# Three norms on row-wide tiles instead of one column per token, in a fused two-block layer (one core)

## The chip, the core and the metric

The kernel runs on one core of a Trainium2 chip. The metric is the device time of one execution in microseconds (us), and lower is better. The engines are named as in the profile: PE (TensorE matmuls), PEld (its weight loads), DVE (VectorE), ACT (ScalarE), POOL (GpSimd) and SP (SyncE, which issues most DMAs).

## The reference, cut to what matters

Two blocks run one after the other on 512 tokens of 1024 features: an RWKV-7 branch beside sparse latent attention, then a convolution, memory attention and gated feed-forward block. The change touches only the start of the attention branch:

```python
def rmsnorm(x, g):
    xf = x.astype(jnp.float32)
    y = xf * lax.rsqrt(jnp.mean(xf * xf, axis=-1, keepdims=True) + NORM_EPS)
    return (y * g.astype(jnp.float32)).astype(x.dtype)
...
    xn = rmsnorm(x, norm_g)
    p = xn @ w_in
...
    c_q = rmsnorm(q_down, q_norm_g)         # 256 features
    c_kv = rmsnorm(kv_down, kv_norm_g)      # 128 features, the latent keys
    q = (c_q @ w_uq).reshape(B, T, ATTN_HEADS, HEAD_DIM)
    q_idx = (c_q @ w_qidx).reshape(B, T, IDX_HEADS, IDX_DIM)
    k_idx = layernorm(k_idx_raw, kidx_g, kidx_b).astype(f32)   # 64 features, the selection keys
```

## The kernel before, in words

Activations lie with features on the 128 partitions and the 512 tokens along the free axis. Every large product is cut into weight units of 1024 x 256, each split into a high and a low part: ACT writes `w_hi` (line 1209), DVE writes `w_lo` (line 1665; for later units POOL does, line 1156), and PE runs three products for each chunk of 128 features (lines 392 to 394). Two slots hold the units in turn. The waits of PE for `hi_ready` and `lo_ready` stand in `next_unit`.

Each engine runs a list written out by hand; semaphores join the lists, and no engine changes its order. Units 0 to 2 (`qd`, `kvi`, `wa`) use the input before its norm; from unit 3 (`r`, half 0) on, the operand is the normed input, made chunk by chunk: DVE scales (line 1692), ACT rounds to the high part (line 1255), DVE subtracts (line 1703). PE takes unit `r` chunk by chunk as these become ready, then computes the selection queries (`index_queries`, line 510), then takes unit 4 (`k`, half 0).

A norm's sum over features is a sum over partitions, which PE must make. `column_sums` (line 433) multiplies the squares, as weights, by a single column of ones, so that the 512 sums come out as 4 columns of 128 tokens on the partitions. DVE scales, adds epsilon and inverts these 128 x 4 numbers (`token_root`, lines 1755 and 1757), ACT takes the root (line 1220), and `spread` (line 383) sends them through PE again, so that each token's factor stands on all partitions. This is done for the query down-projection (`ss_q`, `rs_q`), the latent keys (`ss_kv`, `rs_kv`) and the selection keys (`ki_var`, `rs_ki`). PSUM has 8 banks, which PE takes in a ring.

What stands in the lists near the three norms: on DVE, the norm of the queries is ahead of `split_lo(3)`, the low part of unit `r`; that of the latent keys is ahead of chunks 6 and 7 of the normed input; that of the selection keys is ahead of the scaling of the queries (line 1801) and of `split_lo(4)`, the low part of unit `k`. On ACT, the root of the selection keys is ahead of a tanh and of `split_hi(4)`, the high part of unit `k`.

Of the kernel before, what the change touches and what calls it, by code (L numbers as in the profile page):

```python
# [18 lines left out]
ALU = mybir.AluOpType  # L19
# [3 lines left out]
P = 128  # L23
D = 1024
T = 512
CH = D // P
NT = T // P
HD = 64
# [99 lines left out]
def build(nc, dram, out):  # L128
# [3 lines left out]
    with ctx:  # L132
        base = -(-nc.sbuf_base // 32) * 32

        def at(name, offset, shape, dt=F32):
            return nc.alloc_sbuf_tensor_at(name, [P] + shape, dt, offset=base + offset)
# [22 lines left out]
        R0 = 133504  # L159
# [5 lines left out]
        raw_lo = at("raw_lo", R0 + 16384, [CH, T], F32R)  # L165
        sq_x = at("sq_x", R0 + 32768, [CH, T])

        ar = at("ar", R0, [NI, 2, T])
# [156 lines left out]
        def _(pe):  # L325
# [146 lines left out]
            def third_step(u, m, k):  # L472
                if k == 0:
                    pe.wait_ge(lo_ready, u + 1)
                elif k == 4:
                    pe.wait_ge(sem("sq_q"), 2)
                    column_sums("ss_q", [prep[m][:, 0:T] for m in range(2)])

# [7 lines left out]
            pe.wait_ge(sem("sq_kv"), 1)  # L486
            column_sums("ss_kv", [prep[2][:, 0:T]])
            pe.wait_ge(sem("tok_q_ready"), 1)
            spread("rs_q", tok_rs)

            def index_norms(k):
                pe.wait_ge(sem("xn_ready"), k + 1)
                if k == 4:
                    pe.wait_ge(sem("ki_sq"), 1)
                    column_sums("ki_var", [prep[3][:, 0:T]], slice(0, HD))
                elif k == 5:
                    pe.wait_ge(sem("tok_kv_ready"), 1)
                    spread("rs_kv", tok_mix)
                elif k == 7:
                    pe.wait_ge(sem("tok_ki_ready"), 1)  # L500
                    spread("rs_ki", tok_ki)

# [92 lines left out]
            def attention_start():  # L595
                pe.wait_ge(sem("dsa_w"), 16 * 3)
                for i in range(NI):
                    b = bank(("q", i))
                    for m in range(2):
                        mm = nc.tensor.matmul(b[:, :], wuq[:, m, i * P:i * P + P], qd[:, m, :], start=m == 0, stop=m == 1)  # L600
                    done(mm, ("q", i))
                decay_and_rate(1)
                norms_spread(1)
                strict_upper(0)
                evacuated(pe, "rs_kv")
                transposes("ckv_tok", [ckv[:, t * P:t * P + P] for t in range(NT)])
                for i in range(NI):
                    evacuated(pe, ("q", i))
                absorbed_query(0)
                absorbed_query(1)  # L610
                scores(0)
                key_bonus(1)
# [582 lines left out]
        def _(act):  # L1195
# [69 lines left out]
            hi_chunks((3, 4), "xn")  # L1265
            root(tok_rs, "tok_q_ready")
            hi_chunks((4, 5), "xn")
# [6 lines left out]
            A(prep[3][:, 0:T], kidx[:, :], ACT.Square).then_inc(sem("ki_sq"), 1)  # L1274
            root(tok_mix, "tok_kv_ready")
            hi_chunks((6, CH), "xn")
            root(tok_ki, "tok_ki_ready")
            A(tmp[2][0:32, 0:T], tmp[2][0:32, 0:T], ACT.Tanh).then_inc(sem("tanh_ready"), 1)
# [364 lines left out]
        def _(dve):  # L1643
# [109 lines left out]
            def token_root(key, t, scale, eps, name):  # L1753
# [3 lines left out]
                V.reciprocal(t, t).then_inc(sem(name + "_var"), 1)  # L1757

            token_root("ss_x", rs_x, 1.0 / D, NORM_EPS, "tok_x")
            evacuated(dve, "rs_x")  # L1760
# [13 lines left out]
            for m in range(2):  # L1774
# [4 lines left out]
            input_normed(3)  # L1779
            token_root("ss_q", tok_rs, 1.0 / 256, NORM_EPS, "tok_q")  # L1780
            split_lo(3)
# [10 lines left out]
                 ("wa", 0, 0))  # L1792
            token_root("ss_kv", tok_mix, 1.0 / P, NORM_EPS, "tok_kv")
            input_normed(6)
            input_normed(7)
            lo_chunk(CH - 1, "xn")
            token_root("ki_var", tok_ki, 1.0 / HD, LN_EPS, "tok_ki")
            b = take(dve, "rs_q")
            for m in range(2):
                evacuated(dve, ("qd", 0, m))  # L1800
                ins = V.scalar_tensor_tensor(qd[:, m, :], qd[:, m, :], pcol("q_norm_g", m), b[:, :], ALU.mult, ALU.mult)
                ins.then_inc(sem("cq_ready"), 1)
            dve.wait_ge(sem("cq_ready"), 2)
            release("rs_q")
            split_lo(4)

            def latent_keys():
                evacuated(dve, ("kvi", 0, 0))
                b = take(dve, "rs_kv")
                evac(V.scalar_tensor_tensor(ckv[:, :], ckv[:, :], pcol("kv_norm_g"), b[:, :], ALU.mult, ALU.mult), "rs_kv")  # L1810

            def index_keys():
                evacuated(dve, "ki_mean")
                b = take(dve, "rs_ki")
                evac(V.scalar_tensor_tensor(kidx[:, :], kidx[:, :], pcol("kidx_g"), b[:, :], ALU.mult, ALU.mult), "rs_ki")
                evacuated(dve, "rs_ki")
                V.tensor_scalar(kidx[:, :], kidx[:, :], pcol("kidx_b"), None, ALU.add).then_inc(sem("kidx_ready"), 1)
# [668 lines left out]
```

## Time and profile before

| | us |
|---|---|
| median of 3 runs | 1510.31 (1510.0 to 1523.92) |
| profiled execution | 1511.18 |
| its span, first to last instruction | 1509.4 |
| PE busy | 1448.3 (96%) |
| DVE busy | 980.9 (65%) |
| ACT busy | 497.2 (33%) |
| POOL busy | 489.3 (32%) |

Sums and shares tell of the whole program only. The part that the change touches lies between 36 and 62 us of the span, so it has to be read as a timeline: when each engine started what, and how long it sat idle before. A timeline row gives the start, the time of the row's instructions, engine, source line, operation, tiles and count; in brackets stands the idle time ahead of it, with what ended it. For PE the difference between starts tells more than the durations, since matmuls overlap.

### The profile page before, as it was taken

Reading aid. Unit: us, or ns where it says so; the run is one execution under the profiler, and the core shown is the slowest. Engines: PE = TensorE matmul, PEld = TensorE weight load, DVE = VectorE, ACT = ScalarE, POOL = GpSimd, SP = SyncE. Lnnn points to the kernel's source line nnn. Section 1 sums busy time; section 2 is a strip of 40 time slices with the busy share of each in tenths; the row PEclk is TensorE's granted clock in tenths of the full one; section 3 lists DMA queues with packets and bytes.
Section 4 is the critical chain, followed back from the end, with each engine's and each line's share of the span. In section 5 each row is a group of like instructions: output and inputs, shape, how many; then the busy total and the mean of one; then the engine's idle time right before and its main releaser. Section 6 shows DMA issues by size and latency. Waiting matters only on the chain.

```text
span 1509.4 us, 18586 instructions
## 1 busy us (share of the span) xinstructions
PE 1448.3 (96%) x7552; PEld 1162.8 (77%) x7552; DVE 980.9 (65%) x1393; ACT 497.2 (33%) x674; POOL 489.3 (32%) x132
## 2 busy tenths in 40 slices
PE   8999988899999999999999999989989999999997
PEld 6778654586978787788888887768878888888886
DVE  6679788743563655677996975583247888885121
ACT  5443365452333333122222223322234333332121
POOL 0004021002444422343444443333432434343441
PEclk9999998999998999999999999999999999999998
DMA  5222000111322221223232222212231232323221
GB/s 200 84 84 84 1 2 1 37 50 66 131 86 104 91 84 56 84 84 112 84 103 93 99 97 84 84 66 102 84 112 56 89 107 84 112 84 105 82 93 56
DMA packets 21348, 125.12 MB, mean 83 GB/s; under 512 B 2384, under 2 KB 3408, under 8 KB 7696
## 3 DMA queue, kind: packets, MB, share of 16 engines
q1 hardware_dynamic: 20752, 121.71, 23.0%
q10 hardware_dynamic: 512, 2.23, 0.4%
q8 instruction: 60, 0.98, 0.3%
q14 instruction: 24, 0.20, 0.0%
HBM read 121.84 MB, written 2.10 MB: 82 GB/s over the span
## 4 chain that ended last, share of the span: by engine, by line
PE 87%; DVE 9%; ACT 2%; issue 1%; DMA 0%; POOLq 0%; POOL 0%; DVEq 0%; SPq 0%; ACTq 0%
PE bank L392 24%; PE bank L393 24%; PE bank L394 24%; PE bank L344 1%; PE bank L961 1%; PE bank L977 1%; DVE prob L1970 1%; PE bank L374 1%; DVE m_blk L1992 1%; PE bank L825 1%; DVE tmp L1990 1%; DVE op_lo L1703 1%; ACT w_hi L1209 1%; PE bank L824 1%; DVE conv_b L2349 1%
## 5 line engine op out<-in xcount | busy, mean ns | idle before, releaser
L1156 POOL TENSOR_TENSOR w_lo<-w_raw,w_hi 128x2048 fp32r<-128x2048 f32 (+1 forms) x102 | 466.7, 4575 | 833.2 <-ACT w_hi L1209 811.2
L392 PE MATMUL bank<-op_hi,w_hi 128*128 128x512 f32 x1344 | 531.7, 396 | 13.5 <-DVE op_lo L1682 6.6
L393 PE MATMUL bank<-op_lo,w_hi 128*128 128x512 f32 x1344 | 527.3, 392 | 0.0
L394 PE MATMUL bank<-op_hi,w_lo 128*128 128x512 f32 x1344 | 527.2, 392 | 0.0
L392 PEld LDWEIGHTS bank<-op_hi,w_hi 128*128 128x128 f32 x1344 | 254.4, 189 | 71.7 <-issue 11.3
L1209 ACT ACTIVATE w_hi<-w_raw 128x2048 fp32r<-128x2048 f32 (+2 forms) x109 | 205.7, 1887 | 283.0 <-PE bank L394 283.0
L393 PEld LDWEIGHTS bank<-op_lo,w_hi 128*128 128x128 f32 x1344 | 254.4, 189 | 54.4 <-issue 0.7
L394 PEld LDWEIGHTS bank<-op_hi,w_lo 128*128 128x128 f32 x1344 | 254.1, 189 | 54.4
L2241 DVE SCALAR_TENSOR_TENSOR bank<-pad_b,par,bank 128x512 f32<-128x512 f32 x232 | 175.3, 756 | 7.8
L2408 DVE TENSOR_TENSOR tmp<-tmp,conv_f 128x512 f32<-128x512 f32 x22 | 101.5, 4615 | 16.4 <-ACT tmp L1628 16.4
L2149 DVE TENSOR_TENSOR x_res<-bank,x_res 128x512 f32<-128x512 f32 x24 | 16.5, 691 | 108.8 <-PE bank L394 108.6
L392 PE MATMUL bank<-act_hi,w_hi 128*128 128x512 f32 x176 | 69.4, 394 | 0.0
L394 PE MATMUL bank<-act_hi,w_lo 128*128 128x512 f32 x176 | 69.3, 394 | 0.0
L393 PE MATMUL bank<-act_lo,w_hi 128*128 128x512 f32 x176 | 69.2, 393 | 0.0
L2402 DVE SCALAR_TENSOR_TENSOR conv_f<-bank,par,conv_f 128x511 f32<-128x511 f32 x66 | 49.2, 747 | 11.6 <-ACT conv_f L1624 10.4
L1624 ACT ACTIVATE conv_f<-bank,par 128x512 f32<-128x512 f32 x33 | 22.7, 689 | 101.7 <-PE bank L394 101.7
L2319 DVE TENSOR_TENSOR tmp<-bank,gate 128x512 f32<-128x512 f32 x16 | 11.1, 691 | 68.9 <-PE bank L394 68.8
L1553 ACT ACTIVATE gate<-bank,par 128x512 f32<-128x512 f32 x24 | 16.4, 685 | 73.7 <-PE bank L394 73.7
L394 PEld LDWEIGHTS bank<-act_hi,w_lo 128*128 128x128 f32 x176 | 33.1, 188 | 7.8
L393 PEld LDWEIGHTS bank<-act_lo,w_hi 128*128 128x128 f32 x176 | 33.1, 188 | 7.7
L392 PEld LDWEIGHTS bank<-act_hi,w_hi 128*128 128x128 f32 x176 | 33.1, 188 | 7.6
L2161 DVE TENSOR_TENSOR sq<-sq 128x512 f32<-128x512 f32 x10 | 25.9, 2595 | 16.2 <-ACT sq L1516 9.0
(368 smaller groups left out, 1798.8 us busy)
## 6 DMA issues: line engine op xcount, KB each, us to landing
w_raw<-in_w_units SPq DMA_DIRECT2D x104, 1024.0 KB, 4.8
w_raw<-in_w_units SPq DMA_DIRECT2D x4, 768.0 KB, 4.2
x_res<-in_x SPq DMA_DIRECT2D x8, 256.0 KB, 6.1
x_res<-in_x ACTq DMA_DIRECT2D x2, 1024.0 KB, 7.4
out<-x_res SPq DMA_DIRECT2D x8, 256.0 KB, 2.3
w_raw<-in_w_units SPq DMA_DIRECT2D x3, 512.0 KB, 7.7
w_raw<-in_w_units SPq DMA_DIRECT2D x4, 256.0 KB, 5.8
mem_tok<-in_mem SPq DMA_DIRECT2D x1, 1024.0 KB, 5.8
```

Source lines behind the costliest of these rows:

```text
L392: nc.tensor.matmul(b[:, 0:width], h, xh[:, x0 + k, 0:width], start=start and k == ks[0], stop=False)
L393: nc.tensor.matmul(b[:, 0:width], h, xl(x0 + k, width), start=False, stop=False)
L394: mm = nc.tensor.matmul(b[:, 0:width], l, xh[:, x0 + k, 0:width], start=False, stop=stop and k == ks[-1])
L1156: nc.gpsimd.tensor_tensor(w_lo[u % 2][:, 0:nk, :], w_raw[u % 2][:, 0:nk, :], w_hi[u % 2][:, 0:nk, :].bitcast(F32), ALU.subtract).then_inc( ...
L1209: A(w_hi[u % 2][:, 0:nk, 0:n], w_raw[u % 2][:, 0:nk, 0:n], ACT.Copy).then_inc(hi_ready, 1)
L1553: evac(A(gates[m][:, :], take(act, ("pg", branch, i, m))[:, :], ACT.Sigmoid, bias=pcol("b_gate_2", 8 * branch + 2 * i + m)), ("pg", branch ...
L1624: A(conv_f[i % 2][m][:, 0:T], take(act, ("up", i, m))[:, :], ACT.Copy, scale=pcol("conv_ffn_w_2", 4 * FC + FC * m + i)).then_inc(sem("tap_ ...
L2149: evac(V.tensor_tensor(x, b[:, :], x, ALU.add), (what, i, m))
L2161: ins = V.tensor_tensor(sq[:, 0, :], sq[:, 0, :], sq[:, c, :], ALU.add)
L2241: ins = V.scalar_tensor_tensor(to, pad[:, k:k + T], pcol("conv_b_w_2", 8 * k + i), y, ALU.mult, ALU.add)
L2402: ins = V.scalar_tensor_tensor(y[:, back:T], b[:, 0:T - back], w, y[:, back:T], ALU.mult, ALU.add)
L2408: link(V.tensor_tensor(g, g, y[0][:, 0:T], ALU.mult))
```

## The change

The three sums are now made with a full 128 x 128 matrix of ones as the weights and the squares as the moving operand (one product for the latent keys, two for the queries, and one with the two-block matrix `pair_ones` for the selection keys). So each sum comes out of PE already on all partitions, as 128 x 512 numbers. DVE scales and inverts these 128 x 512 numbers into three new SBUF tiles, ACT takes their root in place, and DVE multiplies by them. The three spreads are gone, with their banks. The place of each norm in each engine's list stays.

```diff
+        norm_q, norm_kv, norm_ki = (at(f"norm_{n}", R0 + 40960 + 2048 * j, [T])[:, :] for j, n in enumerate(("q", "kv", "ki")))
...
                     pe.wait_ge(sem("sq_q"), 2)
-                    column_sums("ss_q", [prep[m][:, 0:T] for m in range(2)])
+                    b = bank("ss_q")
+                    for m in range(2):
+                        mm = nc.tensor.matmul(b[:, :], ones[:, :], prep[m][:, 0:T], start=m == 0, stop=m == 1)
+                    done(mm, "ss_q")
...
             pe.wait_ge(sem("sq_kv"), 1)
-            column_sums("ss_kv", [prep[2][:, 0:T]])
-            pe.wait_ge(sem("tok_q_ready"), 1)
-            spread("rs_q", tok_rs)
+            b = bank("ss_kv")
+            done(nc.tensor.matmul(b[:, :], ones[:, :], prep[2][:, 0:T], start=True, stop=True), "ss_kv")
...
                 if k == 4:
                     pe.wait_ge(sem("ki_sq"), 1)
-                    column_sums("ki_var", [prep[3][:, 0:T]], slice(0, HD))
-                elif k == 5:
-                    pe.wait_ge(sem("tok_kv_ready"), 1)
-                    spread("rs_kv", tok_mix)
-                elif k == 7:
-                    pe.wait_ge(sem("tok_ki_ready"), 1)
-                    spread("rs_ki", tok_ki)
+                    b = bank("ki_var")
+                    done(nc.tensor.matmul(b[:, :], pair_ones[:, :], prep[3][:, 0:T], start=True, stop=True), "ki_var")
...
-                evacuated(pe, "rs_kv")
+                pe.wait_ge(sem("ckv_ready"), 1)
...
-            root(tok_rs, "tok_q_ready")
+            root(norm_q, "row_q_ready")
...
-            root(tok_mix, "tok_kv_ready")
+            root(norm_kv, "row_kv_ready")
             hi_chunks((6, CH), "xn")
-            root(tok_ki, "tok_ki_ready")
+            root(norm_ki, "row_ki_ready")
...
+            def row_root(key, t, scale, eps, name):
+
+                evac(V.tensor_scalar(t, take(dve, key)[:, :], scale, eps, ALU.mult, ALU.add), key)
+                evacuated(dve, key)
+                V.reciprocal(t, t).then_inc(sem(name + "_var"), 1)
...
-            token_root("ss_q", tok_rs, 1.0 / 256, NORM_EPS, "tok_q")
+            row_root("ss_q", norm_q, 1.0 / 256, NORM_EPS, "row_q")
...
-            token_root("ss_kv", tok_mix, 1.0 / P, NORM_EPS, "tok_kv")
+            row_root("ss_kv", norm_kv, 1.0 / P, NORM_EPS, "row_kv")
...
-            token_root("ki_var", tok_ki, 1.0 / HD, LN_EPS, "tok_ki")
-            b = take(dve, "rs_q")
+            row_root("ki_var", norm_ki, 1.0 / HD, LN_EPS, "row_ki")
+            dve.wait_ge(sem("row_q_ready"), 1)
...
-                ins = V.scalar_tensor_tensor(qd[:, m, :], qd[:, m, :], pcol("q_norm_g", m), b[:, :], ALU.mult, ALU.mult)
+                ins = V.scalar_tensor_tensor(qd[:, m, :], qd[:, m, :], pcol("q_norm_g", m), norm_q, ALU.mult, ALU.mult)
```

The latent keys and the selection keys are multiplied by `norm_kv` and `norm_ki` in the same way.

On DVE, the rows around the third norm, from the last chunk of the normed input to the low part of unit `k` (`w_lo_53`), stand so before:

```order
L1703 TENSOR_TENSOR op_lo<-tmp_63,op_hi 128x512 [waits xn_hi,xn_ready]
L1755 TENSOR_SCALAR misc<-bank 128x4 [waits bank_full5,xn_ready]
L1757 RECIPROCAL misc<-misc 128x4 [waits bank_free5]
L1801 SCALAR_TENSOR_TENSOR qd<-qd,par,bank 128x512 [waits bank_free0,bank_full2]
L1801 SCALAR_TENSOR_TENSOR qd<-qd,par,bank 128x512 [waits bank_free1]
L1665 TENSOR_TENSOR w_lo_53<-w_raw_49,w_hi_51 128x2048 [waits cq_ready,bank_full6,w_hi_ready]
```

and so after:

```order
L1701 TENSOR_TENSOR op_lo<-tmp_63,op_hi 128x512 [waits xn_hi,xn_ready]
L1759 TENSOR_SCALAR norm_ki<-bank 128x512 [waits bank_full4,xn_ready]
L1761 RECIPROCAL norm_ki<-norm_ki 128x512 [waits bank_free4]
L1805 SCALAR_TENSOR_TENSOR qd<-qd,par,norm_q 128x512 [waits bank_free0,row_q_ready]
L1805 SCALAR_TENSOR_TENSOR qd<-qd,par,norm_q 128x512 [waits bank_free1]
L1663 TENSOR_TENSOR w_lo_53<-w_raw_49,w_hi_51 128x2048 [waits bank_full6,w_hi_ready,cq_ready]
```

Nothing has moved; the two rows of the norm went from 128x4 to 128x512. On PE, between the last raw unit and the first product of unit `r` (`w_hi_52`), there stood before:

```order
L485 MATMUL bank<-kidx,pair_ones 128x512 [waits bank_free0,bank_free3,consts]
L433 MATMUL bank<-ones,prep_80 128x1 [waits bank_free1,sq_kv]
L433 MATMUL bank<-ones,prep_80 128x1 x3
L383 MATMUL bank<-ident,misc 128x128 [waits bank_free2,tok_q_ready]
L383 MATMUL bank<-ident,misc 128x128 x3
L392 MATMUL bank<-op_hi,w_hi_52 128x512 [waits bank_free4,bank_free3,xn_ready,w_lo_ready,w_hi_ready]
```

and after:

```order
L394 MATMUL bank<-raw_lo,w_hi_51 128x512
L395 MATMUL bank<-raw_hi,w_lo_53 128x512
L489 MATMUL bank<-kidx,pair_ones 128x512 [waits bank_free0,bank_free3,consts]
L492 MATMUL bank<-prep_83,ones 128x512 [waits bank_free1,sq_kv]
L393 MATMUL bank<-op_hi,w_hi_52 128x512 [waits bank_free3,bank_free2,xn_ready,w_lo_ready,w_hi_ready]
```

Here eight small products (x1 and x3, twice) have become one wide one, and unit `r` follows at once. The spread no longer takes a bank, so unit `r` waits for banks 3 and 2 of the ring, where it waited for 4 and 3.

## Rows read from the trace of the kernel before

**Rows 1.** The page: PE's busy time, POOL by slices of 37.7 us, the chain by engine.
```profile
PE 1448.3 (96%) x7552; PEld 1162.8 (77%) x7552; DVE 980.9 (65%) x1393; ACT 497.2 (33%) x674; POOL 489.3 (32%) x132
...
POOL 0004021002444422343444443333432434343441
...
PE 87%; DVE 9%; ACT 2%; issue 1%; DMA 0%; POOLq 0%; POOL 0%; DVEq 0%; SPq 0%; ACTq 0%
```
**Rows 2.** Timeline of PE, 36 to 62 us (start, us, engine, line, operation, count).
```profile
36.57 1.84 PE L433 MATMUL bank<-ones,prep 128*128 128x1 f32 x16
38.27 0.48 PE L392 MATMUL bank<-raw_hi,w_hi 128*128 128x512 f32 x1
...
41.14 1.02 PE L485 MATMUL bank<-kidx,pair_ones 128*128 128x512 f32 x2
42.00 0.95 PE L433 MATMUL bank<-ones,prep 128*128 128x1 f32 x8
42.81 1.14 PE L383 MATMUL bank<-ident,misc 128*128 128x128 f32 x8
43.70 0.47 PE L392 MATMUL bank<-op_hi,w_hi 128*128 128x512 f32 x1
...
45.17 0.40 PE L392 MATMUL bank<-op_hi,w_hi 128*128 128x512 f32 x1
...
46.55 0.39 PE L392 MATMUL bank<-op_hi,w_hi 128*128 128x512 f32 x1
...
57.77 3.60 PE L510 MATMUL bank<-qd,wqi 128*128 128x512 f32 x8
...
61.56 0.47 PE L392 MATMUL bank<-op_hi,w_hi 128*128 128x512 f32 x1
```
**Rows 3.** Timeline of DVE, 38 to 69 us.
```profile
38.52 0.16 DVE L1755 TENSOR_SCALAR misc<-bank 128x4 f32<-128x4 f32 x1 [0.78 <-PE bank L433]
38.72 0.18 DVE L1757 RECIPROCAL misc<-misc 128x4 f32<-128x4 f32 x1
38.82 2.27 DVE L1665 TENSOR_TENSOR w_lo<-w_raw,w_hi 128x2048 fp32r<-128x2048 f32 x1
...
46.57 0.68 DVE L1703 TENSOR_TENSOR op_lo<-tmp,op_hi 128x512 fp32r<-128x512 f32 x1
...
50.52 0.16 DVE L1755 TENSOR_SCALAR misc<-bank 128x4 f32<-128x4 f32 x1 [1.02 <-PE bank L433]
...
50.81 1.39 DVE L1801 SCALAR_TENSOR_TENSOR qd<-qd,par,bank 128x512 f32<-128x512 f32 x2
54.92 2.29 DVE L1665 TENSOR_TENSOR w_lo<-w_raw,w_hi 128x2048 fp32r<-128x2048 f32 x1 [2.71 <-ACT w_hi L1209]
...
68.10 0.75 DVE L1740 SCALAR_TENSOR_TENSOR kt<-bank,par,kt 128x511 f32<-128x511 f32 x1 [4.38 <-ACT kt L1283]
```
**Rows 4.** Timeline of ACT, 50 to 54 us.
```profile
50.93 0.21 ACT L1220 ACTIVATE misc<-misc 128x4 f32<-128x4 f32 x1 [2.22 <-DVE misc L1757]
51.16 1.28 ACT L1278 ACT_TABLE_LOAD   x1
...
52.99 1.90 ACT L1209 ACTIVATE w_hi<-w_raw 128x2048 fp32r<-128x2048 f32 x1
```
**Rows 5.** Timeline of DVE, 956 to 962 us: one 128x512 norm.
```profile
956.56 0.69 DVE L1673 TENSOR_SCALAR rs<-bank 128x512 f32<-128x512 f32 x1 [1.99 <-PE bank L1016]
957.28 3.35 DVE L1675 RECIPROCAL rs<-rs 128x512 f32<-128x512 f32 x1
```
**Rows 6.** ACT's groups by line and shape: the root of a 128x512 row.
```profile
L1220 ACT ACTIVATE rs<-rs 128x512 f32<-128x512 f32 x1 | 0.6, 634 | 4.3 <-DVE rs L1675 4.3
```
**Rows 7.** Stretches, us from the span's start: busy time of each engine, granted clock (PEclk, 1 is 2.4 GHz).
```profile
174.00:177.00 3.00, 0.40 (x2) 0.30 (x2) 2.90 (x5) 2.97 (x5) 0.00 (x0) 1.00 0.00 0
...
230.60:237.40 6.80, 6.11 (x80) 3.46 (x81) 4.95 (x13) 4.34 (x14) 0.94 (x1) 0.50 0.02 4
```
**Rows 8.** Timeline of PE, 220 to 235 us: the gap ahead of that stretch.
```profile
231.29 0.88 PE L645 MATMUL bank<-ar,bt 64*32 64x32 f32 x64 [3.97 <-DVE misc L1960]
```

More of the change, by code:

```diff
@@ L1796, in _ @@
             lo_chunk(CH - 1, "xn")
-            token_root("ki_var", tok_ki, 1.0 / HD, LN_EPS, "tok_ki")
-            b = take(dve, "rs_q")
+            row_root("ki_var", norm_ki, 1.0 / HD, LN_EPS, "row_ki")
+            dve.wait_ge(sem("row_q_ready"), 1)
             for m in range(2):
                 evacuated(dve, ("qd", 0, m))
-                ins = V.scalar_tensor_tensor(qd[:, m, :], qd[:, m, :], pcol("q_norm_g", m), b[:, :], ALU.mult, ALU.mult)
+                ins = V.scalar_tensor_tensor(qd[:, m, :], qd[:, m, :], pcol("q_norm_g", m), norm_q, ALU.mult, ALU.mult)
                 ins.then_inc(sem("cq_ready"), 1)
             dve.wait_ge(sem("cq_ready"), 2)
-            release("rs_q")
             split_lo(4)
@@ L1808, in latent_keys @@
                 evacuated(dve, ("kvi", 0, 0))
-                b = take(dve, "rs_kv")
-                evac(V.scalar_tensor_tensor(ckv[:, :], ckv[:, :], pcol("kv_norm_g"), b[:, :], ALU.mult, ALU.mult), "rs_kv")
+                dve.wait_ge(sem("row_kv_ready"), 1)
+                V.scalar_tensor_tensor(ckv[:, :], ckv[:, :], pcol("kv_norm_g"), norm_kv, ALU.mult, ALU.mult).then_inc(sem("ckv_ready"), 1)
             def index_keys():
                 evacuated(dve, "ki_mean")
-                b = take(dve, "rs_ki")
-                evac(V.scalar_tensor_tensor(kidx[:, :], kidx[:, :], pcol("kidx_g"), b[:, :], ALU.mult, ALU.mult), "rs_ki")
-                evacuated(dve, "rs_ki")
+                dve.wait_ge(sem("row_ki_ready"), 1)
+                link(V.scalar_tensor_tensor(kidx[:, :], kidx[:, :], pcol("kidx_g"), norm_ki, ALU.mult, ALU.mult))
                 V.tensor_scalar(kidx[:, :], kidx[:, :], pcol("kidx_b"), None, ALU.add).then_inc(sem("kidx_ready"), 1)
```

## The prediction

> **What bounds the kernel now.** I read the page first. PE is busy in 96% of the span and holds 87% of the chain that ended last; DMA has none of it [rows 1]. So a change counts by what it does to PE's next start. The averages don't say what DVE or ACT does to PE in the 26 us that are touched, so next came the timelines of PE, DVE and ACT there. PE has no gap in them: after the last raw product it makes the small sums at 42.00, a spread at 42.81, starts unit `r` at 43.70 and takes a chunk each 1.38 us (45.17 to 46.55); the selection queries start at 57.77 and unit `k` at 61.56 [rows 2]. DVE runs close ahead of it. The low part of unit `r` ends at 38.82 + 2.27 = 41.09, 2.6 before PE needs it, and that of unit `k` at 54.92 + 2.29 = 57.21, 4.35 before [rows 2, 3]. The latter waited for ACT's high part, which started at 52.99, behind the selection keys' root (50.93) and the tanh [rows 4]. These leads are what the change has to spend.
>
> **The PE side of the change.** The queries' one-column sums took 38.27 - 36.57 = 1.70 us. Their replacement is two products of the kind of the row at 41.14 (f32, 128x512, two passes), which takes 42.00 - 41.14 = 0.86: 1.72, no difference. The latent keys' sum goes from 0.81 to 0.86. The spread at 42.81 took 0.89 and goes, with two like it (I take 0.8 each, nearer to the 0.81 of the eight small products before it) [rows 2]. In all PE has 2.4 us less to do, if it has its operands.
>
> **The DVE side.** A norm on 128x4 numbers costs 0.20 (38.52 to 38.72) and 0.10 (38.72 to 38.82), since the next instruction starts before the short one's recorded end: 0.30 in all [rows 3]. The change makes it 128x512 numbers, and the trace has one such norm, in the second block: 957.28 - 956.56 = 0.72 for scaling out of PSUM, then a reciprocal of 3.35, of which I take off the same 0.08 of overlap, 3.27 [rows 5]. That is 3.99 for 0.30: **3.69 us more on DVE for each of three norms**, 11.1 in all. I take this row as it is: its shapes and PSUM source are the same. POOL shows 0 in the slice from 38 to 75 us [rows 1], so nothing there competes with DVE.
>
> The Trainium skill speaks against the change too (VectorE: DVE Perf Modes, "First, the fixed hardware budget"): it says that reciprocal is an iterative divide with a repeat count of 8. An estimate from that page, eight times the scaling pass of 0.69 us, would be 5.5 us a reciprocal and 6.5 us more in all; the measured 3.35 decides.
>
> **What of this reaches PE.** Three places, in order.
>
> First norm, ahead of the low part of unit `r`. That ends at 41.09 + 3.69 = 44.78. PE would be free at 42.00 + 0.86 = 42.86 and has to wait until about 44.9: 1.2 us later than the 43.70 of before, where it could have been 0.8 earlier.
>
> Second norm, ahead of chunks 6 and 7. The subtraction that completes the sixth chunk ended at 46.57 + 0.68 = 47.25 [rows 3]; with two norms it ends at 47.25 + 7.38 = 54.6. PE has done five chunks and the selection keys' sum by 44.9 + 6.90 + 0.86 = 52.7, so it waits some 2.0 us more, and with three chunks left is through unit `r` at about 58.8 (before, 57.77).
>
> Third norm. DVE idled 1.02 us ahead of it for PE's small sums [rows 3]; now DVE is the late one, so this idle time goes and the delay at its end is 3 x 3.69 - 1.02 = 10.05. Two things are queued behind. On DVE, the scaling of the queries: it ended at 50.81 + 1.39 = 52.20 and now ends at 62.25. PE waits for it from 58.8, a gap of 3.5 us, and is through the selection queries (61.56 - 57.77 = 3.79) at 66.1. On ACT, the root, the tanh and the high part of unit `k`: the root starts 10.05 later and is 128x512, 634 ns for 210 [rows 4, 6], so the high part starts at 52.99 + 10.05 + 0.4 = 63.45. The low part follows: 57.21 + 10.45 = 67.65, and PE starts unit `k` at about 67.75, not 61.56. **The sum is 10.05 + 0.4 - 4.35 + 0.1 = +6.2 us.** The other chain (66.1) is 1.6 shorter, so it costs nothing more. With unit `k`'s lead spent, the 2.4 us that PE saves lie inside its waits and are worth nothing.
>
> **After unit `k`.** Nothing gives the 6.2 back: PE is the bound from there on, and weights load only as slots are freed by engines that are late by the same amount. Nothing adds to it either. DVE is 10 us late at 55, but idled 2.71 ahead of the low part and 4.38 at 68.10 [rows 3], and its first use of unit `k` comes one tile, 24 products of 0.23, after PE's start. Fewer banks taken by the spreads shift the ring; the order is the same, so each product still waits for a bank used eight takes ago. I cost this at nothing; if a reuse did bite, it would be by one eviction, 0.7.
>
> Against the profiled execution: 1511.18 + 6.2 = 1517.4. That execution is 0.9 above the median of the runs, so the median would be 1516.5. I add half a microsecond for the clock (below): **1517**.
>
> **Rivals.**
>
> 1. *The clock falls in the new gaps.* PE idles 2.0 us, 3.5 and then 1.6. In a stretch with 0.40 us of PE work in 3 the clock stays at 1.00 [rows 7]; after an idle time of 3.97 [rows 8] 6.8 us at 0.50 (1.2 GHz) follow [rows 7]. The gap of 3.5 lies between and is nearer to the second. If the clock falls there, the selection queries need twice their 3.79, from 62.35 to 69.9, which is 2.2 past the start of unit `k`; at most, a stretch of 6.8 us at half clock does 3.4 us less work. That gives 6.2 + 2.2 = +8.4, up to +9.6: 1519 to 1520. The Trainium skill (TensorE: Matmul & The Clock Gate, "HAM oscillation — how this bites in real kernels") says that idle gaps between bursts bring the half clock back and that the work after them pays. The rows here show that for the longer gap and not for the shorter. Chance 0.27.
>
> 2. *DVE's cover holds, and only PE's saving counts.* If the reciprocals took no longer than the scaling pass of 0.72, DVE would be 3 x (1.44 - 0.30) - 1.02 = 2.4 late at unit `k`, less than the lead of 4.35, and PE would be 2.4 faster: 1508. For it: PE really has less to do. Against it: the reciprocal row of 3.35 is of just this shape. It decides below about 1.2 us a reciprocal, where 3 x 0.72 + 3r - 0.9 - 1.02 + 0.4 reaches 4.35 (r = 1.24). Chance 0.02.
>
> 3. *Part of it is hidden.* The third norm starts before I think, or PE's wait for chunk six is shorter, and the lead of 4.35 is larger by an instruction or two: +3 to +4.5, 1514 to 1515. Chance 0.12.
>
> 4. *Slower by over 1%.* That takes 15 us. The delay shifts all later work, and the clock's falls with it; four more stretches like that of 6.8 us at half speed, at 3.4 each, would be 13.6 on top of 6.2: 1530. PE is busy in most later stages, so so many are unlikely: 0.03.
>
> **The numbers.** The forecast itself (1515.5 to 1518.5) has 0.56. The low end takes in case 3, the high end case 1 and one later half-speed stretch of 1.7 or so: 1513.5 to 1521.5. A measurement of this kernel can tell about 1%, 15 us, from no change. Cases 1 and 3 and the forecast all lie within that: so does case 2 (0.2% faster). Slower is case 4 and 0.01 for what I have not seen, 0.04; faster is such a 0.01 alone; 0.95 is left for within 1%.
>
> **What would show it.** In the timeline of DVE three reciprocals of about 3.35 us between 38 and 62 us, each after a scaling of 0.7; unit `r`'s low part ends near 44.8, unit `k`'s near 67.7. On PE: unit `r` starts near 44.9, a gap of some 2 us before its sixth chunk, one of 3.5 before the selection queries, one of 1.6 before unit `k`, which starts near 67.75 after DVE's low part. From there every row of before stands about 6 us later. The granted clock between 59 and 70 us tells case 1. It would be wrong if the reciprocals were much shorter, if unit `k` started before 65, or if later waits of PE grew or shrank by more than the shift.

## The result, and the profile after

| | before | changed |
|---|---|---|
| median (10 executions each) | 1511.72 us | 1530.23 us |
| lowest to highest | 1509.30 to 1526.35 | 1519.37 to 1533.24 |
| profiled execution, its span | 1511.18, 1509.4 | 1530.71, 1529.0 |
| granted clock, mean over the span | 0.977 | 0.966 |

The ratio is 1.0082, with an interval from 1.0047 to 1.0116: slower by 0.8%, or 7 to 18 us, which is clear of the scatter. The medians are 18.5 us apart, 1.2%. The forecast was 1517.0 with a range up to 1521.5, so the median lies 13 us beyond the forecast and 9 beyond the range. The executions of either kernel lie at separate levels: of 164 executions of the kernel before that were made for this study, 95 lie about a mean of 1510.9 and 69 about 1524.7. The mean over all is 1516.7, and the three runs that the prediction started from happened to have a median at the lower level.

In the touched stretch the forecast held. DVE after, 38 to 69 us (answers to [rows 3]):

```profile
38.46 0.69 DVE L1759 TENSOR_SCALAR norm_q<-bank 128x512 f32<-128x512 f32 x1 [0.82 <-PE bank L480]
39.18 3.35 DVE L1761 RECIPROCAL norm_q<-norm_q 128x512 f32<-128x512 f32 x1
42.45 2.23 DVE L1663 TENSOR_TENSOR w_lo<-w_raw,w_hi 128x2048 fp32r<-128x2048 f32 x1
...
49.94 3.35 DVE L1761 RECIPROCAL norm_kv<-norm_kv 128x512 f32<-128x512 f32 x1
...
57.48 3.35 DVE L1761 RECIPROCAL norm_ki<-norm_ki 128x512 f32<-128x512 f32 x1
60.75 1.31 DVE L1805 SCALAR_TENSOR_TENSOR qd<-qd,par,norm_q 128x512 f32<-128x512 f32 x2
65.32 2.29 DVE L1663 TENSOR_TENSOR w_lo<-w_raw,w_hi 128x2048 fp32r<-128x2048 f32 x1 [3.26 <-issue]
```

The low part of unit `r` ends at 42.45 + 2.23 = 44.68 (forecast 44.78), that of unit `k` at 65.32 + 2.29 = 67.61 (forecast 67.65). ACT between them, 58 to 66 us (answers to [rows 4]):

```profile
60.86 0.63 ACT L1218 ACTIVATE norm_ki<-norm_ki 128x512 f32<-128x512 f32 x1 [4.94 <-DVE norm_ki L1761]
61.51 1.28 ACT L1276 ACT_TABLE_LOAD   x1
...
63.34 1.89 ACT L1207 ACTIVATE w_hi<-w_raw 128x2048 fp32r<-128x2048 f32 x1
```

PE after, 41 to 69 us (answers to [rows 2]; an idle time in brackets is PE's own, with what ended it):

```profile
41.83 1.02 PE L492 MATMUL bank<-prep,ones 128*128 128x512 f32 x2
44.78 0.47 PE L393 MATMUL bank<-op_hi,w_hi 128*128 128x512 f32 x1 [1.93 <-issue]
...
54.52 0.50 PE L393 MATMUL bank<-op_hi,w_hi 128*128 128x512 f32 x1 [0.17 <-DVE op_lo L1701]
...
62.16 5.37 PE L508 MATMUL bank<-qd,wqi 128*128 128x512 f32 x8 [3.23 <-DVE qd L1805]
67.37 0.60 PE L345 MATMUL bank<-ident,tmp 128*128 128x128 f32 x4
67.72 0.47 PE L393 MATMUL bank<-op_hi,w_hi 128*128 128x512 f32 x1
```

Unit `r` starts at 44.78 (44.9), unit `k` at 67.72 (67.75), 6.16 later than before (61.56). The queries took 5.2 (62.16 to 67.37) instead of 3.4 (57.77 to 61.20), since the clock fell in that place. With the transposes behind them they were over just when DVE's low part was there (67.61), so nothing came on top. The local step is 6.2, as forecast. The other 13.3 us of the two profiled executions arose later. In the stretches view (us from the span's start, length, busy time and count on PE, PEld, DVE, ACT, POOL, granted clock, DMA share, GB/s) of the changed kernel stand the two places with a low clock near the norms, and two stages far behind them:

```profile
46.00:49.40 3.40, 3.40 (x10) 2.66 (x9) 3.37 (x6) 1.35 (x2) 0.00 (x0) 0.51 0.71 287
63.10:66.50 3.40, 3.40 (x6) 1.33 (x5) 1.18 (x1) 3.40 (x5) 0.00 (x0) 0.50 0.01 2
...
302.40:312.70 10.30, 8.76 (x160) 7.84 (x150) 4.79 (x8) 3.73 (x7) 0.00 (x0) 0.67 0.60 218
312.70:429.80 117.10, 112.83 (x1001) 92.80 (x999) 46.76 (x68) 42.23 (x72) 22.73 (x5) 0.91 0.17 63
```

and of the same two stages of the kernel before:

```profile
294.20:300.90 6.70, 5.63 (x160) 5.07 (x150) 4.80 (x8) 3.52 (x7) 0.00 (x0) 1.00 0.43 134
300.90:410.30 109.40, 105.15 (x1001) 87.93 (x999) 46.63 (x68) 42.04 (x72) 22.72 (x5) 0.98 0.21 80
```

The first stage is that of the many 32x32 and 64x64 products that invert the diagonal blocks (lines 745 to 760), from DVE's last masking of `g_k` to its first copy of `z`; I call it the *block products*. The second runs from there to the first normalised output of the RWKV state's recurrence; I call it the *recurrence*. Both do the same work in the two kernels, with as many instructions, and have a lower clock after. Stage by stage:

| us | to first use of `k` on DVE | to block products | block products | recurrence | rest | span |
|---|---|---|---|---|---|---|
| before | 68.1 | 226.1 | 6.7 | 109.4 | 1099.1 | 1509.4 |
| changed | 74.3 | 228.1 | 10.3 | 117.1 | 1099.1 | 1529.0 |
| difference | 6.2 | 2.0 | 3.6 | 7.7 | 0.0 | 19.6 |

Two thirds of the difference, 13.3 us, arise in stages that the change does not touch, and in all three of them more time passes at half clock: 27.3 us instead of 23.9 up to the block products (1.7 of the 2.0 there; a second trace of the changed kernel, `e13_after_again`, has 23.9 and 227.0), 6.8 instead of 0 in them, 20.5 instead of 3.4 in the recurrence. The experiments had to tell whether the change causes that, and by what.

### The profile page after: what moved, and what is told of

It is laid out like the page before. It is cut to its first block, busy times and chain, and to the rows that moved or that the text cites. A ratio compares the mean times of both kernels' runs of the same rounds, so it can differ in the third digit from the quotient of the medians.

```text
span 1529.0 us, 18486 instructions
## 1 busy us (share of the span) xinstructions
PE 1460.7 (96%) x7504; PEld 1166.8 (76%) x7504; DVE 991.1 (65%) x1393; ACT 498.4 (33%) x674; POOL 489.7 (32%) x132
## 3 DMA queue, kind: packets, MB, share of 16 engines
q10 hardware_dynamic: 512, 2.23, 0.4%
## 4 chain that ended last, share of the span: by engine, by line
PE 86%; DVE 10%; issue 2%; ACT 2%; DMA 0%; POOLq 0%; POOL 0%; DVEq 0%; SPq 0%; ACTq 0%
PE bank L393 24%; PE bank L395 24%; PE bank L394 24%; PE bank L345 1%; PE bank L959 1%; PE bank L975 1%; DVE op_lo L1701 1%; PE bank L823 1%; DVE prob L1972 1%; PE bank L375 1%; DVE m_blk L1994 1%; DVE tmp L1992 1%; PE bank L822 1%; ACT w_hi L1207 1%; PE bank L852 1%
## 5 line engine op out<-in xcount | busy, mean ns | idle before, releaser
L1551 ACT ACTIVATE gate<-bank,par 128x512 f32<-128x512 f32 x24 | 16.3, 685 | 73.7 <-PE bank L395 73.7
```

The source lines that it names most:

```text
L1551: evac(A(gates[m][:, :], take(act, ("pg", branch, i, m))[:, :], ACT.Sigmoid, bias=pcol("b_gate_2", 8 * branch + 2 * i + m)), ("pg", branch ...
```

## The experiments

The theories were: **load**, DVE's 11 us of reciprocals are late and delay all that follows; **banks**, fewer takes of the ring shift later waits; **stream**, PE's list has become shorter (7552 passes before [rows 1], 7504 after), so that later instructions stand elsewhere in it; **lot**, any kernel draws its clock anew. Beside a median I give the mean with its standard error, and from each execution's span and granted clock two parts of it: span x clock (the *full-clock part*), and span x (1 - clock) (*lost*). Before, over 154 executions, these are 1474.3 ± 0.1 and 40.9 ± 0.7; changed, over 22 in two sets, 1478.3 ± 0.5 and 47.2 ± 1.6, with a mean of 1527.2 ± 1.3.

### The load alone, and the load taken away

`e1_dve_load` and, on another occasion, `e18_dve_load_again`: the kernel before, with an unused wide norm beside each small one.

```diff
 evac(V.tensor_scalar(t, take(dve, key)[:, 0:NT], scale, eps, ALU.mult, ALU.add), key)
 evacuated(dve, key)
+if key != "ss_x":
+    link(V.tensor_scalar(dummy[:, :], rs[:, :], scale, eps, ALU.mult, ALU.add))
+    link(V.reciprocal(dummy[:, :], dummy[:, :]))
```

> The kernel before, with one 128x512 scaling and one 128x512 reciprocal added on DVE inside each of the three norms (into a tile nobody reads), PE and banks as before: some 3.8 us a norm, where the change adds 3.69. Theory A (the reciprocals make the change's loss, and the delay itself brings more stretches of half clock later): unit k starts near 68 us instead of 61.56, and the executions lie at 1520 to 1531, like those of the change. Theory B (the loss after unit k comes from PE's changed instructions or banks): unit k near 68 as well, but executions at about 1517 with half clock as before (clock 0.976).

> e1_dve_load once more (the kernel before with the DVE time of the change and its own PE stream), for more executions. Theory D: idle time ahead of the small products 0.4 to 1.1 us, mean near the 1521.5 of the first twelve, below the 1526 to 1527 of the changed kernel. Theory C (the delay of unit k alone makes the whole loss): mean 1526.

Measured: medians 1518.1 and 1529.8, means 1521.5 ± 1.8 and 1528.3 ± 1.9, ratios 1.0054 (1.0020 to 1.0088) and 1.0048 (1.0008 to 1.0088). Taken alone, the first set speaks for theory B of its expectation and the second, of the same kernel, for theory C of its own: twelve executions do not settle a few microseconds here. Together, 24 executions: mean 1524.9 ± 1.5, full-clock part 1479.8 ± 0.3, lost 43.3 ± 1.7. DVE in `e1_dve_load`:

```profile
57.68 3.35 DVE L1760 RECIPROCAL dummy<-dummy 128x512 f32<-128x512 f32 x1
...
65.26 2.29 DVE L1666 TENSOR_TENSOR w_lo<-w_raw,w_hi 128x2048 fp32r<-128x2048 f32 x1 [2.71 <-ACT w_hi L1210]
```

and PE:

```profile
64.93 4.21 PE L511 MATMUL bank<-qd,wqi 128*128 128x512 f32 x8
...
69.34 0.48 PE L393 MATMUL bank<-op_hi,w_hi 128*128 128x512 f32 x1
```

The load alone gives the low part of unit `k` at 67.55, as in the changed kernel. PE starts the unit only at 69.34, for it also has the third spread to do (61.58, behind the late root) and the last products of unit `r` after it, and 3.4 us at half clock from 62.8; so the first use of `k` is at 75.9, 7.8 later than before and not 6.2. The load adds 5.5 us of full-clock part and 8.2 ± 1.6 to the mean, where the changed kernel adds 10.5 ± 1.4: what is measured is this delay and nothing clearly beyond it.

`e2_short_recip`: the changed kernel, with the reciprocals on 4 of 512 columns (the factors of the other columns are left without their inversion).

```diff
-V.reciprocal(t, t).then_inc(sem(name + "_var"), 1)
+V.reciprocal(t[:, 0:NT], t[:, 0:NT]).then_inc(sem(name + "_var"), 1)
```

> The changed kernel with each of the three reciprocals over the first 4 of the 512 columns only (the other columns are not inverted). Theory A: the loss goes, unit k starts near 59 us (the 2.4 us that PE saves), executions near 1508 to 1510. Theory B (PE's side or the banks cause the later loss): unit k near 59, but executions at 1515 or above with a clock of 0.970 or lower.

Measured: median 1522.7, ratio 1.0036 (0.9999 to 1.0073), mean 1521.2 ± 1.6, full-clock part 1471.1, lost 48.4.

```profile
51.94 0.18 DVE L1761 RECIPROCAL norm_ki<-norm_ki 128x4 f32<-128x4 f32 x1
52.04 1.40 DVE L1805 SCALAR_TENSOR_TENSOR qd<-qd,par,norm_q 128x512 f32<-128x512 f32 x2
56.62 2.29 DVE L1663 TENSOR_TENSOR w_lo<-w_raw,w_hi 128x2048 fp32r<-128x2048 f32 x1 [3.19 <-issue]
```

Without the load, PE's saving is real: first use of unit `k` at 65.6, 2.5 before that of the kernel before, and 3.2 less of full-clock part. But as much is lost to the clock as in the changed kernel, and the time is not lower. The load is not the whole cause.

`e4_late_start`: the kernel before, with a memset and 3.5 unused reciprocals at the head of DVE's list, far from the norms.

```diff
+link(V.memset(tmp[0][:, 0:T], 1.0))
+for _ in range(3):
+    link(V.reciprocal(tmp[0][:, 0:T], tmp[0][:, 0:T]))
+link(V.reciprocal(tmp[0][:, 0:240], tmp[0][:, 0:240]))
```

> The kernel before with some 6 us of unused reciprocals at the head of DVE's list, so that the whole program, PE's first product included, comes about 6 us later and nothing else differs. If a delay alone shifts the work against the stretches in which the clock falls and so brings more of them, executions lie at 1520 to 1531 as for the change. If not, they lie 5 to 6 above the kernel before, at 1516 to 1517.

Measured: six executions, ratio 1.0105 (1.0044 to 1.0166), full-clock part 1481.1, lost 47.4. The first use of unit `k` is 7.5 later. A delay that has nothing to do with the norms gives the same picture; with six executions it tells no more.

### The banks

`e3_banks_only` and `e8_banks_again` (the same kernel), `e7_banks_by_two`: the kernel before, with PE's ring turned as in the changed kernel (5 on, which in a ring of 8 is the same as its 3 takes fewer, and 8 back where one bank leaves the ring, so that it stays 3 behind), or by 2. `e5_banks_back` and `e6_short_banks_back`: the changed kernel and `e2_short_recip` (so again without most of the inversion), turned back by 3.

```diff
 index_queries()
+turn[0] += 5        # e3, e8; 2 in e7; 3 in e5, e6
...
 ring.remove(CONV_BANK)
+turn[0] -= 8        # e3, e8; 2 in e7
```

> The kernel before with PE's ring of banks advanced by five ahead of unit k, so that from there on every product has the bank it has in the changed kernel; nothing else. Theory A: no change, 1510 to 1512, clock 0.976. Theory B, if it is the banks: half clock and executions of 1520 or above with no delay at unit k (61.6).

> The changed kernel with PE's ring of banks advanced by three ahead of unit k, so that from there on every product has the bank that it had before the change. In the group so far, kernels with shifted banks were at the long level (some 13 us longer, clock 0.965 to 0.968 instead of 0.975 and above) in 24 of 34 executions, those with the banks of before in 15 of 51. Theory B (banks): most executions at 1517 to 1519, the median there. Theory C (chance of how the clock's falls meet the work, whatever the banks): like the changed kernel, half or more at 1529 to 1533.

> The changed kernel with the reciprocals over 4 columns only (the others are not inverted) and the banks of before from unit k on. Theory B (banks): the long level becomes rare, median near 1508, 2.4 below the kernel before. Theory C: as e2_short_recip, median about 1522 with most executions at 1515 to 1525.

> The kernel before with the ring advanced by two instead of five from unit k on. Theory B: if any other assignment of banks brings the long level, most executions at 1521 to 1528. Theory C: about a third, as for the kernel before; median 1510 to 1512.

> e3_banks_only once more (the kernel before with the banks of the changed one), for more executions: it had 7 of 12 at the long level where the kernel before had 10 of 29. Theory B: again more than half, and the two together clearly above the kernel before. Theory C: about a third.

Measured: `e3` and `e8` have medians of 1523.1 and 1523.2, which looked like the banks being the cause; `e7` has 1512.3. But their ratios to the kernel before, which ran beside them, are 1.0027 (0.9984 to 1.0071), 1.0011 and 0.9993, full-clock parts 1473.7 to 1474.2, and together, 36 executions, a mean of 1518.4 ± 1.2 and 42.8 ± 1.4 lost. Turning the banks back doesn't help the changed kernel: `e5` 1525.1 ± 0.9, ratio 1.0050 (1.0018 to 1.0082); `e6` 1523.1 ± 1.6, against 1521.2 of `e2`. These two are not clean tests, though: with the ring turned back, PE waits 2.3 us for a bank that DVE still reads (`ar`) ahead of unit `k`, at 70.08 in `e5`, and the full-clock parts are 3.5 and 2.8 higher. So an order of banks can cost more than the 0.7 that the prediction allowed for a reuse; the order of the changed kernel, in `e3` and `e8`, does not. The banks fall. What had misled was the median of a kernel with two levels: it jumps by 13 us as the share at one level passes a half.

### The place in PE's instruction list

All traces show one wait in the middle of the block products whose releaser is "issue". Timelines of PE before

```profile
295.93 0.22 PE L745 MATMUL bank<-inv_dia,z 32*32 32x32 f32 x2 [1.07 <-issue]
```

and in the changed kernel

```profile
305.11 0.21 PE L743 MATMUL bank<-inv_dia,z 32*32 32x32 f32 x2 [1.54 <-issue]
```

The products there follow each other within hundredths of a microsecond, and packets of the queue of instructions (q8) land in the same stretch; so I took the wait for one on instructions, of a length that depends on the place in PE's list. The DMA records of the traces bear this out: in all twenty, a packet of 16 KB of q8 starts 0.2 to 2.0 us before PE stops, and PE goes on 1.3 to 1.6 us after the packet's end, however long the wait is. Before, the packet lasts from 293.07 to 294.44 and the wait from 294.86 to 295.93; in the changed kernel it lasts from 302.76 to 303.69 and the wait from 303.57 to 305.11. In the twelve traces with a short wait PE stops 1.3 to 2.0 us after the packet's start, in the eight with a long one 0.2 to 1.0 us after it. Unused 32x32 products shift it; 24 of them make 48 passes, as many as the change removed. They stand in `key_bonus(1)`, at 201 us, and in `e14_pad_early` in PE's wait before the selection queries:

```diff
 b = bank(("bonus", i))
+if i == 1:
+    for _ in range(24):        # 24 in e9, e11, e17; 12 in e15; 40 in e10; 64 in e16
+        nc.tensor.matmul(b[0:BLK, 0:BLK], ones[0:BLK, 0:BLK], ones[0:BLK, 0:BLK], start=True, stop=True)
```

`e9_pad24`, `e14_pad_early` and `e15_pad12` are the changed kernel with them, `e11_short_pad24` is `e2_short_recip`, `e10_before_pad40` and `e16_before_pad64` the kernel before; `e13_after_again` is the changed kernel once more. `e12_ln_exp_on_act`, with `e17_ln_exp_pad24`, moves the norm to ACT: DVE neither scales nor inverts.

```diff
+def ln_exp(key, t, scale, c, done):
+    act.wait_ge(sem("eps_set"), 2)
+    evac(A(t, take(act, key)[:, :], ACT.Ln, scale=scale, bias=misc[:, c:c + 1]), key)
+    evacuated(act, key)
+    A(t, t, ACT.Exp, scale=-0.5).then_inc(sem(done), 1)
...
-root(norm_q, "row_q_ready")
+ln_exp("ss_q", norm_q, 1.0 / 256, 99, "row_q_ready")
...
-row_root("ss_q", norm_q, 1.0 / 256, NORM_EPS, "row_q")
```

> The changed kernel with 24 products of 32x32 (48 passes, 48 weight loads) that nobody reads, in PE's wait for the second key bonus near 180 us: as many PE instructions as the change takes out, so that from there on each instruction stands at the same place of PE's stream as before. Theory D (the shorter stream makes PE wait 1.5 to 2.2 us for instructions in the run of small block products, L743/L745, near 300 us, and the clock falls behind it): the idle time there goes back to 0.4 to 1.1 us, the stretch from the head of the mask products to the first copy of z (8.8 to 10.5 us with the changed stream, 6.1 to 6.7 before) to 6 to 7, and the mean over executions to about 1522, 6 above the kernel before. Theory C (chance alone): idle time and stretch as in the changed kernel, mean 1525 to 1527.

> The kernel before with 40 such products at the same place (160 instructions, about 1 us of work in a wait). Theory D, if it is where in the stream the run of small products lies: 160 more or 96 fewer are the same place modulo 256 instructions of 64 bytes, the size of the 16 KB blocks in which the trace shows instructions arriving, so the idle time rises to 1.5 to 2.2 us and the stretch to 9 or 10, mean 3 above the kernel before. Theory C: 0.4 to 1.1 and 6 to 8 us, mean as before.

> The changed kernel with the reciprocals over 4 columns only (the other columns are not inverted) and the 24 products of e9_pad24. Theory D: the idle time near 297 us falls below 1.1, and the mean goes from the 1522 of e2_short_recip and e6_short_banks_back to about 1514, 2.4 below the kernel before. Theory C: about 1522 again.

> The changed kernel with the inverse root made on ACT, out of PSUM, as exp(-0.5 ln(mean + eps)) and nothing of it on DVE. Each norm then has two table loads of 1.28 us and two passes of 0.6 on ACT in place of 3.99 us on DVE. If what counts is the chain to unit k's low part: norms cost 3.7 us each on ACT, which idles more there; unit k starts at 61 to 62 us instead of 67.7, and the mean lies 5 to 6 below the changed kernel, at 1520 to 1521.

> The changed kernel itself once more, for more executions and a second trace. Theory D (the change's stream makes PE wait for instructions near 300 us and the clock fall behind it): idle time ahead of L743 1.5 to 2.2 us, mean 1525 to 1527. Theory C (chance): the mean over these executions comes down to about 1522, the 6 us of the reciprocals above the kernel before.

> The changed kernel with the 24 unused products in PE's wait for the scaled queries near 60 us instead of near 180: same count, another place. Theory D: idle time near 300 us at 0.4 to 1.1 us as with the pad near 180 (1.0 there, 0.8 with short reciprocals), mean about 1523. Theory C: unlike e9_pad24 it goes back to 1.5 or more.

> The changed kernel with 12 unused products (48 instructions, half of what the change takes out) near 180 us. Theory D: an idle time between, some 1.2 to 1.6 us, if it grows steadily with the distance; mean 1523 to 1527. Theory C: no order in the idle times of the paddings 0, 12 and 24.

> The kernel before with 64 unused products near 180 us: 256 instructions, one whole block of 16 KB at 64 bytes each. Theory D: the run of small products lies at the same place of a block as in the kernel before, so the idle time returns from the 1.8 us of 40 products to 0.4 to 1.1; mean 1 to 3 above the kernel before for the pad's own work. If it only grows with the number of instructions, 2 us or more.

> e12_ln_exp_on_act (the inverse root on ACT) with the 24 unused products near 180 us. In the trace of e12 the first use of unit k comes 1.8 us earlier than in the kernel before, but the idle time ahead of the small block products is 1.9 us and half clock follows. Theory D: with the pad the idle time is 0.4 to 1.1 us and the executions lie 1 to 2 us below the kernel before level by level (1509 and 1523), mean 1515 to 1516, which is not to be told from the kernel before. Theory C: as e12, mean 1519.

Each profiled execution, by its stages. "Wait" is that on issue. The two columns "at" need a word: in every trace the stretches at half clock start at the points of one even grid, within 0.02 us. "At" is where in this grid the stage starts, as the time since the last point. In brackets, the time at half clock in the stage.

| | wait | at | block products | at | recurrence | rest | span |
|---|---|---|---|---|---|---|---|
| before | 1.1 | 2.15 | 6.7 (0) | 2.06 | 109.4 (3.4) | 1099.1 | 1509.4 |
| e3 | 0.7 | 2.43 | 6.4 (0) | 1.98 | 109.4 (3.4) | 1099.2 | 1508.2 |
| e7 | 0.5 | 2.41 | 6.2 (0) | 1.78 | 109.4 (3.4) | 1099.1 | 1507.4 |
| e11 | 0.8 | 2.20 | 6.5 (0) | 1.83 | 109.4 (3.4) | 1099.2 | 1509.6 |
| e1 | 0.4 | 2.25 | 6.1 (0) | 1.50 | 123.0 (34.1) | 1099.1 | 1528.7 |
| e18 | 0.4 | 2.40 | 6.1 (0) | 1.65 | 123.0 (34.1) | 1099.0 | 1528.2 |
| e14 | 0.7 | 2.19 | 6.3 (0) | 1.71 | 123.0 (34.1) | 1099.1 | 1528.5 |
| e17 | 0.4 | 2.33 | 6.1 (0) | 1.57 | 123.0 (34.1) | 1099.2 | 1519.1 |
| e8 | 0.8 | 0.60 | 8.1 (3.4) | 1.84 | 109.4 (3.4) | 1099.1 | 1509.1 |
| e9 | 1.0 | 0.45 | 8.3 (3.4) | 1.92 | 109.4 (3.4) | 1099.3 | 1519.5 |
| e16 | 0.7 | 0.76 | 7.9 (3.4) | 1.86 | 109.4 (3.4) | 1099.2 | 1515.0 |
| e4 | 0.6 | 0.64 | 7.8 (3.4) | 1.61 | 123.0 (34.1) | 1099.1 | 1533.6 |
| e5 | 1.6 | 2.41 | 8.8 (3.4) | 0.99 | 107.9 (0) | 1102.1 | 1522.4 |
| e10 | 1.8 | 2.14 | 9.1 (3.4) | 0.96 | 107.9 (0) | 1102.0 | 1516.3 |
| e12 | 1.9 | 2.22 | 9.1 (3.4) | 1.11 | 107.9 (0) | 1100.7 | 1508.4 |
| e6 | 2.1 | 2.40 | 9.4 (3.4) | 1.54 | 122.9 (34.1) | 1099.1 | 1525.8 |
| e13 | 1.9 | 2.43 | 9.1 (3.4) | 1.33 | 123.0 (34.1) | 1099.2 | 1532.5 |
| after | 1.5 | 0.36 | 10.3 (6.8) | 0.46 | 117.1 (20.5) | 1099.1 | 1529.0 |
| e2 | 1.7 | 0.38 | 10.5 (6.8) | 0.68 | 117.0 (20.5) | 1099.1 | 1520.3 |
| e15 | 1.8 | 0.33 | 10.6 (6.8) | 0.71 | 117.0 (20.5) | 1099.1 | 1528.9 |

**The wait.** Its length follows the place in PE's list, in all twenty. That 40 pads on the list of before would make it long and 64 short again was put down ahead of `e10` and `e16`. It is 0.4 to 1.1 with the list of before and of its variants with other banks or more DVE work, again with the changed list and 24 pads at either place, and with the list of before and 64 pads. It is 1.5 to 2.1 with the changed list, with half of the pads, and with 40 pads on the list of before. Each time it is 1.5 or more, the block products have 3.4 us more at half clock than those that start at the same place with the shorter wait (3.4 for 0 at 2.1 to 2.4, 6.8 for 3.4 at 0.3 to 0.8), and are some 2.6 us longer in full. The rest of the 3.6 of the first pair goes with where the stage starts: with the short wait it takes 6.1 to 6.7 from 2.1 to 2.4 and 7.8 to 8.3 from 0.4 to 0.8, which is why `e9` has 8.3 where 6 to 7 was expected. In rows, the changed kernel with the pads (`e9_pad24`), to be held against the 302.40 row of the changed kernel above:

```profile
302.50:310.80 8.30, 7.25 (x159) 6.48 (x149) 4.80 (x9) 3.63 (x7) 0.00 (x0) 0.79 0.53 198
```

and its wait:

```profile
304.20 0.21 PE L746 MATMUL bank<-inv_dia,z 32*32 32x32 f32 x1 [1.05 <-issue]
```

**The recurrence.** It has four lengths and no others, and they are told apart by where it starts in the grid of clock changes: 0.46 to 0.71, 117.0; 0.96 to 1.11, 107.9; 1.33 to 1.71, 123.0; 1.78 to 2.06, 109.4. No trace breaks the order, whatever its edit, and `e14` and `e16` both start the stage at 306.4 us of the span and still differ by 13.6. In three traces, those with 107.9, the rest is 1.6 to 3.0 us longer; in the other seventeen the rest is 1099.0 to 1099.3. The stretches view of `e17_ln_exp_pad24`:

```profile
290.90:296.90 6.00, 5.61 (x156) 5.05 (x147) 4.76 (x8) 3.52 (x7) 0.00 (x0) 1.00 0.47 153
296.90:419.90 123.00, 118.74 (x1000) 97.14 (x999) 46.80 (x68) 42.28 (x72) 22.75 (x5) 0.86 0.19 71
```

and of `e5_banks_back`:

```profile
303.60:312.40 8.80, 7.21 (x159) 6.38 (x148) 4.77 (x9) 3.74 (x7) 0.00 (x0) 0.81 0.54 188
312.40:420.30 107.90, 103.63 (x1000) 86.39 (x998) 46.70 (x69) 42.18 (x72) 22.79 (x5) 1.00 0.20 74
```

Same products, 15.1 us apart. This fits the two levels of the kernel before: 1524.7 - 1510.9 = 13.8, and 123.0 - 109.4 = 13.6. It fits in the parts too: executions at the upper level lose 16.3 us more to the clock (50.1 against 33.8), and 30.7 us more at half clock in the recurrence make 15.4. But no execution of that kernel at its upper level was profiled, so that its recurrence takes 123.0 there is inferred. The relation was read from the traces after the last run; no experiment moved the start of the stage alone, so it is a regularity of twenty traces, not a cause that was switched on and off.

**The times.** `e9` 1526.8 ± 2.5 and `e14` 1525.7 ± 2.1 are not below the changed kernel's 1527.2 ± 1.3, though it was expected that pads would bring it down; `e15` has 1524.7 ± 1.5. Without the DVE load the pads seem to help, 1517.8 ± 1.5 (`e11`, `e17`) against 1521.0 ± 1.0 (`e2`, `e6`, `e12`), a difference of 3.2 ± 1.8. On the kernel before, `e10` (long wait) lies above `e16` (short, with more pads), 1523.6 ± 1.0 to 1521.3 ± 2.1. `e18`, with the load and the short wait in its trace, has 1528.3 ± 1.9, as much as the changed kernel. A gain of 2.6 is of the size of these errors, and the lot of the recurrence lies on top, so the price of the wait stands on the stages of the traces and not on the times.

**Inverting on ACT.** `e12` has ratio 1.0018 (0.9980 to 1.0056), `e17` 0.9988 (0.9948 to 1.0029); both together a mean of 1518.4 ± 1.4. ACT in `e12`, one norm:

```profile
51.02 1.28 ACT L1236 ACT_TABLE_LOAD   x1
52.31 0.69 ACT L1236 ACTIVATE norm_ki<-bank,misc 128x512 f32<-128x512 f32 x1
53.02 1.28 ACT L1238 ACT_TABLE_LOAD   x1
54.31 0.63 ACT L1238 ACTIVATE norm_ki<-norm_ki 128x512 f32<-128x512 f32 x1
```

Unit `k` is first used 1.8 us before that of the kernel before, and the full-clock part is 1.8 lower (1472.5 ± 0.3), in spite of two table loads a norm. In time it can't be told from the kernel before. No version beats both kernels.

## Why the prediction was wrong

- **The PE side, the DVE side and the three places**: right. Reciprocals of 3.35 us thrice, PE's saving of 2.4 (2.5 in `e2`), unit `r` at 44.78 for 44.9, the queries' gap 3.23 for 3.5, unit `k` +6.16 for +6.2. The Trainium skill's repeat count (VectorE: DVE Perf Modes, "First, the fixed hardware budget"), from which 5.5 us a reciprocal was estimated, is not borne out here by any of the three. The wait ahead of chunk six was 0.17, not 2.0, since the clock had fallen at 46.0, behind PE's idle time of 1.93, and PE reached the chunk late by itself.
- **Rival 1** came true as a mechanism (half clock from 63.1 to 66.5, behind the gap of 3.23) and cost nothing. It went wrong in its size: the transposes at 67.37 were over at about the moment when DVE's low part (67.61) was, so the slower queries filled the 1.6 us that PE would have waited anyway. That it came out at nothing is luck: in `e1` the half clock in the same place helped to bring unit `k` 1.6 later.
- **"After unit `k`. Nothing gives the 6.2 back ... Nothing adds to it either"**: this step failed. Nothing is given back, but 13.3 us were added in the profiled pair, 2.0 up to the block products, 3.6 in them and 7.7 in the recurrence. Rival 4 named the mechanism ("the clock's falls with it") and got 0.03, on the ground that PE is busy in most later stages. Busy time does not carry that: in the 109.4 us of the recurrence before, PE counts 105.15 as busy, and the same stage has 34.1 us at half clock in seven other traces. The half-clock stretches at 230.6 [rows 7] should have been read as one draw, not as a fixed cost. In all, the changed kernel's trace has 33.4 us more at half clock, where rival 4 had four stretches of 6.8, or 27.2. That its 1530 is the measured median is luck all the same: it was added to an execution at the lower level, and the kernel before goes 13.8 up without any change.
- **The reference**: the sum was made against 1511.18, an execution at the lower level. Of the three runs shown, one was at 1523.92; that alone said that the kernel has a second level 13 us up. Against the mean of 1516.7, the term of 6.2 alone would have given 1523, and the 2.6 of the block products 1525.5, with 1527.2 ± 1.3 measured.

What the whole +10.5 ± 1.4 of the mean consists of, then: 6.2 of delay from the reciprocals, read in the trace and shown as a cause by `e1` and `e18` (7.8 of delay there, +8.2 ± 1.6 in the mean) and, from the other side, by `e2`; about 2.6 from the longer wait in the block products, shown stage by stage and not in the times; and the rest, 1.7 ± 1.4, is no more than its error. The median moved by 18.5 because it also changed levels: 95 of 164 executions of the kernel before lie below 1517, and of the changed kernel 8 of 22 at its lower level (1518 to 1522.2), the others at 1526 to 1540. Open stay whether that share differs other than by chance, and what in the recurrence decides by tenths of a microsecond of its start.

## What to carry to other kernels

A 128x512 fp32 reciprocal on DVE costs as much as five scaling passes; before a per-token norm is widened to spare PE small products, count whether DVE's lead over PE can pay for it, for the saving on PE lies in its waits once the lead is gone. Where the first few runs show two values of a time, take the mean over many, name the stage that differs, and put the other level into the range: in these traces a shift by some microseconds, or by a few instructions of PE's list, went with another level. Costs should be compared stage by stage between traces, since a stage untouched by the change that has the same work and another clock shows at once which part of a difference is not the edit's own.

## What was not expected of the hardware

- The same 1,001 products of the recurrence take 107.9, 109.4, 117.0 or 123.0 us, with 0, 3.4, 20.5 or 34.1 us at 1.2 GHz, in traces whose edits all lie elsewhere, ordered by the start of the stage alone, and PE counts as busy in some 96% of each. The Trainium skill (TensorE: Matmul & The Clock Gate, "HAM oscillation — how this bites in real kernels") has idle gaps between bursts bring the half clock back; here up to 34.1 us, about a third of a trace's half clock, stand in a stage in which PE's longest idle time is 0.93 us, in all twenty traces.
- In dense runs of 32x32 products PE waits for "issue" once, for 0.4 to 2.1 us. The wait depends on how many instructions stand before the place: 24 small products added 100 us earlier gave 1.0 instead of the 1.5 and 1.9 of the changed kernel's two traces, and 12 did not shorten it (1.8). It ends 1.3 to 1.6 us after a 16 KB packet of the instruction queue.
